# Second feed-forward product as seven quadrant products, with weight sums made by adding DMAs

## The reference

```python
f = jnp.square(jax.nn.relu(h @ w_ff1[l])) @ w_ff2[l]
h = layer_norm(DEEPNORM_ALPHA * h + f, ln2_g[l], ln2_b[l])
```

## Time and profile before

| | us |
|---|---|
| runs | 1128.21 median of 3 (1127.84 to 1128.37) |
| the profiled execution | 1128.61 |
| its span, first to last instruction | 1126.8 |
| PE busy | 1110.5 (99%) |
| DVE busy | 593.9 (53%) |
| ACT busy | 418.8 (37%) |
| POOL busy | 66.6 (6%) |

### The profile page before, as it was taken

How to read it: one execution, slowest core, us unless ns; L and a number is a source line. 1 busy time by engine, 2 the same in 40 slices (tenths; PEclk the granted TensorE clock), 3 DMA queues, 4 the chain that set the end, 5 groups by cost and what they waited for, 6 DMA issues and landing times.

```text
span 1126.8 us, 13004 instructions
## 1 busy us (share of the span) xinstructions
PE 1110.5 (99%) x5404; PEld 931.6 (83%) x5404; DVE 593.9 (53%) x672; ACT 418.8 (37%) x446; POOL 66.6 (6%) x87
## 2 busy tenths in 40 slices
PE   8999999999999999999999999999999999999996
PEld 8788888887888888888888888888888888888885
DVE  5553357556455475559565646586333234445446
ACT  7444342543433522343424633333223224232330
POOL 3000000000022000002000000131000000000002
PEclk9999999999999999999999999999999999999998
DMA  8523421223233532222322221442332322323211
GB/s 273 193 78 112 136 72 55 84 75 112 78 109 125 156 113 75 75 94 76 112 68 65 93 75 41 174 159 75 112 112 74 112 87 100 112 74 112 87 62 75
DMA packets 82737, 114.79 MB, mean 102 GB/s; under 512 B 4316, under 2 KB 57948, under 8 KB 82560
## 3 DMA queue, kind: packets, MB, share of 16 engines
q1 hardware_dynamic: 79648, 103.19, 28.4%
...
## 4 chain that ended last, share of the span: by engine, by line
PE 90%; DVE 5%; POOL 2%; issue 1%; ACT 1%; DMA 0%; DVEq 0%; POOLq 0%; SPq 0%
PE bank L369 27%; PE bank L371 27%; PE bank L370 27%; PE bank L477 2%; PE bank L671 1%; DVE bn L1466 1%; POOL rstd_tmp L1784 1%; POOL rstd L1785 1%; DVE residual L1602 1%; DVE w_lo L1162 1%; PE bank L597 1%; PE bank L578 1%; PE bank L727 1%; PE bank L630 1%; PE bank L615 1%
## 5 line engine op out<-in xcount | busy, mean ns | idle before, releaser
L1162 DVE TENSOR_TENSOR w_lo<-w_raw,w_hi 128x2048 fp32r<-128x2048 f32 (+1 forms) x92 | 205.3, 2233 | 276.9 <-ACT w_hi L871 274.7
L369 PE MATMUL bank<-act_t_hi,w_hi 128*128 128x512 f32 (+1 forms) x832 | 320.2, 385 | 1.8 <-ACT u_gelu L1048 1.3
L371 PE MATMUL bank<-act_t_hi,w_lo 128*128 128x512 f32 (+1 forms) x832 | 317.2, 381 | 0.0
L370 PE MATMUL bank<-act_t_lo,w_hi 128*128 128x512 f32 (+1 forms) x832 | 317.0, 381 | 0.0
L871 ACT ACTIVATE w_hi<-w_raw 128x2048 fp32r<-128x2048 f32 (+1 forms) x91 | 172.0, 1892 | 204.2 <-PE bank L371 192.4
L369 PEld LDWEIGHTS bank<-act_t_hi,w_hi 128*128 128x128 f32 x832 | 156.5, 188 | 32.1 <-issue 2.3
L371 PEld LDWEIGHTS bank<-act_t_hi,w_lo 128*128 128x128 f32 x832 | 156.4, 188 | 30.4
L370 PEld LDWEIGHTS bank<-act_t_lo,w_hi 128*128 128x128 f32 x832 | 156.5, 188 | 29.5 <-issue 0.2
L369 PE MATMUL bank<-w_hi,x_hi 128*128 128x512 f32 x416 | 162.2, 390 | 0.0
L371 PE MATMUL bank<-w_hi,x_lo 128*128 128x512 f32 x416 | 161.9, 389 | 0.0
L370 PE MATMUL bank<-w_lo,x_hi 128*128 128x512 f32 x416 | 161.8, 389 | 0.0
...
## 6 DMA issues: line engine op xcount, KB each, us to landing
w_raw<-in_w_in SPq DMA_DIRECT2D x46, 1024.0 KB, 5.2
w_raw<-in_w_ff SPq DMA_DIRECT2D x32, 1024.0 KB, 5.2
w_raw<-in_w_out SPq DMA_DIRECT2D x10, 1024.0 KB, 5.1
w_raw<-in_w_mem_kv SPq DMA_DIRECT2D x3, 1024.0 KB, 6.7
residual<-in_x SPq DMA_DIRECT2D x4, 512.0 KB, 9.6
...
out<-residual SPq DMA_DIRECT2D x3, 512.0 KB, 2.6
```

The lines of the kernel that those rows point to most:

```text
L369: pe.matmul(dst, lh, rh, start=start, stop=False)
L370: pe.matmul(dst, lh, rl, start=False, stop=False)
L371: return pe.matmul(dst, ll, rh, start=False, stop=stop)
L1162: return dve.tensor_tensor(dst, src, hi.bitcast(f32), ALU.subtract)
```

## The change

The first product stays as it is. The second one is done in a Strassen form. The 4096 hidden features are cut into four sections s of 1024; in each, A (512 x 1024) and B (1024 x 1024) are cut into quadrants, A by token halves m and feature halves k, B by feature halves k and column halves n. Per section seven products of quadrants (256 x 512 by 512 x 512) stand in the place of eight. With S1 = A21 - A22, S2 = A11 - S1, S4 = A12 - S2 and S3 = A22 - S2 they are

```diff
+QUADS = 4
+PRODUCTS = 7 * QUADS
+M1, M5, M6, M4, M3, M7, M2 = range(7)
+M_BANK = {M1: 2, M5: 4, M6: 6, M4: 0, M3: 2, M7: 4, M2: 6}
+LN2_ORDER = (2, 3, 0, 1)
...
-    tm("ff2", w_ff2, 0, D, range(8))
...
+    S2 = at("hidden_sum_2", [P, QUADS, 4, 256], XS + 16 * K1)
+    L2G = at("ln2_g_all", [P, D], XS + 16 * K1)
+    L2B = at("ln2_b_all", [P, D], XS + 20 * K1)
+    MH = [WH[0], at("w_hi3", [P, 2048], XS, f32r), WH[1]]
+    ML_ = [WL[0], at("w_lo3", [P, 2048], XS + 8 * K1, f32r), WL[1]]
+    MRAW = RAW + [at(f"w_raw{i}", [P, 2048], TURNED + 8 * K1 * (i - 2)) for i in (2, 3)]
+    MX = [A + 80 * K1, TURNED + 16 * K1, TURNED + 24 * K1]
+    MXH = [at(f"hidden_hi{i}", [P, 4, 256], o, f32r) for i, o in enumerate(MX)]
+    MXL = [at(f"hidden_lo{i}", [P, 4, 256], o + 4 * K1, f32r) for i, o in enumerate(MX)]
...
+        down = a["w_ff2_2"][0].rearrange("(s k q p) (n c) -> s k n p q c", p=P, q=4, k=2, n=2)
+        def four_chunks(t):
+            return t[:, :].rearrange("p (k c) -> p k c", k=4)
+        def hidden(s, m, k):
+            return F1[:, 2 * s + k, :].rearrange("p (q m t) -> p q m t", q=4, m=2)[:, :, m, :]
+        def left_of(i, s):
+            if i == M6:
+                return S2[:, s, :, :]
+            m, k = {M1: (0, 0), M5: (1, 0), M4: (1, 1), M3: (0, 0), M7: (1, 1), M2: (0, 1)}[i]
+            return hidden(s, m, k)
...
+            def product_tile(p, t):
+                i, s = divmod(p, QUADS)
+                key, slot = ("ff2", i, t), p % 3
+                wh, wl = four_chunks(MH[slot]), four_chunks(ML_[slot])
+                dst = take(M_BANK[i] + t, key) if s == 0 else bank[M_BANK[i] + t]
+                for kk in range(4):
+                    last = three(dst[:, :], MXH[slot][:, kk, tile_of(t)], MXL[slot][:, kk, tile_of(t)], wh[:, kk, :], wl[:, kk, :],
+                                 s == 0 and kk == 0, s == QUADS - 1 and kk == 3)
+                if s == QUADS - 1:
+                    give(last, key)
+                return last
+            def product_ready(p):
+                pe.wait_ge(w_lo, ff2_0 + p + 1)
+                pe.wait_ge(x_lo, E_FF2 + p + 1)
+            for p in range(PRODUCTS - 2):
+                product_ready(p)
+                product_tile(p, 0)
+                last = product_tile(p, 1)
+                if p % QUADS < QUADS - 1:
+                    n_used[0] += 1
+                    last.then_inc(w_used, 1)
+                    product_done[p] = (w_used, n_used[0])
                 else:
-                    n_used[0] += 6
-                    tm_pair(n0 + 7, 8, e0 + 6, 3)
+                    b, u = turn["ff2", p // QUADS, 1]
+                    product_done[p] = (bank_full[b], u + 1)
+            for t in range(2):
+                for p in (PRODUCTS - 2, PRODUCTS - 1):
+                    product_ready(p)
+                    product_tile(p, t)
...
+            def right_hi(p):
+                i, s = divmod(p, QUADS)
+                if i in (M1, M3, M2):
+                    act.wait_ge(quad_raw[s], 16 * (1 + (M1, M3, M2).index(i)))
+                else:
+                    act.wait_ge(quad_sum[s], 16 * (1 + (M5, M6, M4, M7).index(i)))
+                act.wait_ge(*(product_done[p - 3] if p >= 3 else block_done[(ff1_0 + 14, WO2 + 3, ff1_0 + 15)[p]]))
+                act.activation(MH[p % 3][:, :], MRAW[s][:, :], ACT.Copy).then_inc(w_hi, 1)
+            def left_hi(p):
+                i, s = divmod(p, QUADS)
+                if i == M1: act.wait_ge(f1_done, 8 * s + 4)
+                if i == M5: act.wait_ge(hidden_sums, 2 * s + 1)
+                if i == M6: act.wait_ge(hidden_sums, 2 * s + 2)
+                if i == M3: act.wait_ge(hidden_sums, 2 * QUADS + s + 1)
+                if i == M7: act.wait_ge(hidden_sums, 3 * QUADS + s + 1)
+                if p:
+                    act.wait_ge(*(product_done[p - 3] if p >= 3 else block_done[ff1_0 + 15]))
+                act.activation(MXH[p % 3][:, :, :], left_of(i, s), ACT.Copy).then_inc(x_hi, 1)
...
+            right_hi(0)
+            left_hi(0)
+            right_hi(1)
             relus(15, 7)
...
+            left_hi(1)
+            for p in range(2, PRODUCTS):
+                left_hi(p)
+                right_hi(p)
...
+            def sums_one_two(s):
+                dve.wait_ge(f1_done, 8 * (s + 1))
+                a21 = hidden(s, 1, 0)
+                dve.tensor_tensor(a21, a21, hidden(s, 1, 1), ALU.subtract).then_inc(hidden_sums, 1)
+                dve.wait_ge(hidden_sums, 2 * s + 1)
+                dve.tensor_tensor(S2[:, s, :, :], hidden(s, 0, 0), a21, ALU.subtract).then_inc(hidden_sums, 1)
+            def sum_four(s):
+                dve.wait_ge(hidden_sums, 2 * QUADS)
+                dve.tensor_tensor(hidden(s, 0, 0), hidden(s, 0, 1), S2[:, s, :, :], ALU.subtract).then_inc(hidden_sums, 1)
+            def sum_three(s):
+                dve.tensor_tensor(hidden(s, 1, 1), hidden(s, 1, 1), S2[:, s, :, :], ALU.subtract).then_inc(hidden_sums, 1)
...
+            def fold(i, t, *quadrants):
+                key = ("ff2", i, t)
+                b = full(dve, key)
+                for m, n, op in quadrants:
+                    ins = dve.tensor_tensor(rows(m, n, t), rows(m, n, t), b[:, :], op)
+                free(ins, key)
+                drained(dve, key)
...
+            def fold_one(t):
+                key = ("ff2", M1, t)
+                b = full(dve, key)
+                for m, n, op in ((0, 0, ALU.add), (0, 1, ALU.subtract), (1, 0, ALU.add), (1, 1, ALU.subtract)):
+                    ins = dve.scalar_tensor_tensor(rows(m, n, t), rows(m, n, t), ALPHA, b[:, :], ALU.mult, op)
+                free(ins, key)
+                drained(dve, key)
...
+            for m in range(16):
+                if m < 14:
+                    squares(m, m // 2)
+                    split(ff1_0 + m + 2)
+                elif m == 14:
+                    squares(m, m // 2)
+                    right_lo(0)
+                    left_lo(0)
+                    right_lo(1)
                 else:
-                    split(n0 + 7)
-                    split_x(1, e0 + 7, F1[:, 7, :])
-                    split(n0 + 8)
-                    split_x(0, e0 + 8, F1[:, 0, :])
-                    for j in range(TT):
-                        add_half(n0, 0, ALPHA, j)
-                        half_stats(RES, j, 0)
-            dve.wait_ge(ln2_in, 32)
-            for j in range(TT):
-                center_rows(ff2_0 + 8, j, L2G, 2 * TT)
-                scale_rows(j, MT + TT + H + 4 * TT, L2B, TT, h2_done, 2 if j == TT - 1 else 1)
+                    squares(m, m // 2)
+                if m % 4 == 3 and m < 15:
+                    sums_one_two(m // 4)
+            left_lo(1)
+            sums_one_two(QUADS - 1)
+            for p in range(2, PRODUCTS):
+                left_lo(p)
+                right_lo(p)
+                i, s = divmod(p, QUADS)
+                if i == M1 and s >= 2: sum_four(s - 2)
+                if i == M5 and s >= 2: fold_one(s - 2)
+                if i == M6 and s >= 2:
+                    sum_four(s)
+                    fold(M5, s - 2, (0, 1, ALU.add), (1, 1, ALU.add))
+                if i == M4 and s >= 2: fold(M6, s - 2, (0, 1, ALU.add), (1, 0, ALU.subtract), (1, 1, ALU.add))
+                if i == M4 and s == 3: sum_three(0)
+                if i == M3 and s >= 2: fold(M4, s - 2, (1, 0, ALU.add))
+                if i == M3 and s < 3: sum_three(s + 1)
+                if i == M7 and s >= 2:
+                    fold(M3, s - 2, (0, 1, ALU.add))
+                    half_stats(RES, s - 2, 1)
+                if i == M2 and s >= 2:
+                    fold(M7, s - 2, (1, 0, ALU.subtract), (1, 1, ALU.add))
+                    half_stats(RES, s, 0)
+                    last_stats(s, 1)
+            last_norm(2)
+            last_norm(3)
+            for t in range(2):
+                fold(M2, t, (0, 0, ALU.add))
+                last_stats(t, 0)
+                last_norm(t, t + 1)
...
+            def add_block(i, s, k, n):
+                pool.wait_ge(w_lo, ff2_0 + QUADS * i + s + 1)
+                pool.dma_start(four_chunks(MRAW[s]), down[s, k, n], accum_op=ALU.add).then_inc(quad_sum[s], 16)
+            for s in range(QUADS): add_block(M1, s, 0, 1)
+            for s in range(QUADS): add_block(M5, s, 1, 1)
+            for s in range(QUADS): add_block(M6, s, 1, 0)
+            for s in range(QUADS): add_block(M3, s, 0, 1)
+            pool.wait_ge(hidden_sums, 4 * QUADS)
...
+            def load_quad(s, k, n):
+                sp.dma_start(four_chunks(MRAW[s]), down[s, k, n]).then_inc(quad_raw[s], 16)
+            for s in range(QUADS):
+                if s < 2:
+                    sp.wait_ge(w_lo, ff1_0 + 15 + s)
+                else:
+                    sp.wait_ge(*block_done[ff1_0 + 15])
+                load_quad(s, 0, 0)
+            for s in range(QUADS):
+                sp.wait_ge(w_lo, ff2_0 + QUADS * M4 + s + 1)
+                load_quad(s, 1, 1)
```

(26 more changed lines are left out.)

115 lines of the change are left out of this document (22 added, 93 removed).

## The result

The changed kernel takes **1116.38 us** (median of 4 runs, 1115.83 to 1117.18), against 1128.29 us for the kernel before beside it on the same chip. The ratio is 0.9891 with a 95% interval of 0.9874 to 0.9908: it is faster by 1.1%, about 12 us. The forecast was 1113.0, with a range of 1105 to 1140 and 0.70 on faster. Sign and kind were right, the size was 3.4 us too good.

A forecast was written before the change was run, and what follows sets the result against it. The prediction took TensorE, busy 99% of the span, as the bound. From 1128.6 us it took 21.8 for matmuls, added 4.8 for the late load and 1.8 at the end: 1113.4, as a median 1113.0 us; range 1105 to 1140.

The forecast's parts named there:

- Matmuls, -21.8: Second feed-forward product on PE: 672 matmuls in place of 768, 96 fewer at 0.2267 us each, 21.8 us less.
- ACT and DVE, nothing on PE: Second product: DVE's excess of 4.3 us in all stays inside the 5.4 us lead, costing PE nothing.
- F: Rival: DVE becomes the bound if half-size operands cost more; no gain, or 1117 to 1122 us; 0.05 faster, 0.04 no change.
- The late load, +4.8: Product 2 of the second product: buffer 2's load shares DMA engines with adds, so PE waits 4.8 us.
- T: DMA engine time of one weight add, taken as 6.3 us, two loads' engine time; bounds 3.2 to 10.2.
- The forecast's own upper end: Upper bound of PE's wait at product 2, with a load landing of 12.9 us: 6.3 us.
- Rival B: Rival: adds cost like plain loads, so PE's stall at product 2 is 0.6 us; 1108.8 us; chance 0.09.
- C: Rival: adds a bit slower, 6.6 to 7.6 us each; 1119 us at 7; chance 0.09.
- D: Rival: twelve adds in a row bind, PE waits at products 4 to 15, kernel slower (1143 us at 9 each); chance 0.20.
- Their own pace: Adds for products 4 to 15: stall of 2.4 us by the twelfth, inside the 4.8 already paid.
- E: Rival: POOL writes DMA requests only between DVE's instructions, so adds act as 8.6 us each; 1138 us; chance 0.06.
- The end, +1.8: After the last matmul: DVE begins the last tile 3.2 us late, not 1.5, adding 1.8 us; bounds -1.5 to +3.

## Why the prediction was right, and where it was off

- **Matmuls, -21.8: right.** Count and 0.2267 us as forecast.
- **ACT and DVE, nothing on PE: right.** Half-size operands took 1.22 us, folds 0.68, as priced; DVE is busy for 24.4 of 30 us (81%) in the densest part, and PE has no wait for it but the one at product 2. F is out.
- **The late load, +4.8: the mechanism was right, a term was too small.** The pause is 6.55, at the place and on the chain given. What failed is "So the load of buffer 2 waits for as many add packets as it has itself: 3.16 + T + 1.9". That gave 11.4 for a landing of 12.9, and a smaller T can't be the reason. The load waited for 749 add packets and not 528: 293 went through before its first packet, the other 456 beside it. DMA from 947 to 951 in the changed kernel:

```profile
q0 software_dynamic: 244, 0.50, 70.3%
q1 hardware_dynamic: 219, 0.45, 35.0%
```

  From its first packets on the load goes nearly one to one with the adds, as the earlier trace rows had it. But 749 packets at the adds' pace (3325 in 33 us) are 7.4 us, where the forecast had 6.3, and q1 moved 955 packets and not 528, since the load of buffer 3 went beside that of buffer 2; at 200 packets a us (799 in 4 us) that is 4.8 and not 3.16. Together 12.2 of the 12.9 us. The first packet is late beside one add as well (2.0 us behind the issue) and beside plain copies (2.4), and about 1 us behind the issue with the engines idle. Why, no run settles: it stays open. The forecast's own upper end, taken from the landing of 12.9 us in the earlier trace rows, was 6.3: the plain reading of a measured landing came nearer than the sum.
- **The clock, missing: +3.0.** This is the step that failed: the forecast priced PE's pause at its length and went on at 0.2267 us. All of the earlier trace rows were at full clock with waits of at most 1.0 us, so they held no price for it; only the last slice of the clock row, an 8 where PE falls idle, could have raised the question.
- **T = 6.3: near.** By the measure the prediction named (the packets' time) it is 5.83; by the pace at which they go through it is 5.1 to 5.24. The forecast's 6.3 was two loads' packets' time; at the pace of plain loads (400 GB/s, measured with all adds gated) two loads of 1.05 MB are 5.2. Rival B's T of 3.2 was too low, C and D (over 6.6) too high. The adds landed 8.5 to 15.0 us after their issue, where 8 to 17 stood. Their own pace cost nothing. D is real as a mechanism: in the version with copies of 0.5 MB PE stops at each product, 6.28 us per add.
- **E: out.** An add takes 5.24 us, not 8.6, beside a DVE at 81%. POOL's issue costs 1.28 us for an add and 0.75 for a plain copy, not 0.81, and is hidden, as said.
- **The end, +1.8: too dear, +0.3.** DVE begins the last tile 2.1 us behind the last matmul, not 3.2, and from tile to tile it is 4.75 us, not 4.96, since the wait for POOL's root is 0.51 and not 0.79.

Put together: 1113.4 + 1.75 (pause) + 3.0 (clock) - 1.5 (end) - 0.8 (earlier start) = 1115.9 for the profiled execution, which took 1116.0. The end, priced too dear, and the earlier start hid 2.3 us of the 4.75 that the pause and the clock cost more than forecast. That the total came within 3.4 us is in part this luck: the late load as it was, clock included, cost 9.5 us where 4.8 stood.
